# Moving z's gate into the next head's steps, and the key's sum of squares to two rounded passes

## The reference, cut to what matters

```python
def l2_normalize(x):
    return x * lax.rsqrt(jnp.sum(jnp.square(x), axis=-1, keepdims=True) + NORM_EPS)
def gated_deltanet_branch(qkv, z, b, a, conv_w, a_log, dt_bias, norm_g):
    ...
    qkv = jax.nn.silu(causal_depthwise_conv(front(qkv.astype(f32)), conv_w.astype(f32)))
    q, k, v = jnp.split(qkv, [GDN_QK, 2 * GDN_QK], axis=-1)
    ...
    k = l2_normalize(k.reshape(B, Lp, GDN_HEADS, GDN_DK))
    ...
    o = chunked_gated_delta_rule(bhl(q), bhl(k), bhl(v), bhl(g), bhl(beta))
    ...
    o = rms_norm(o, norm_g) * jax.nn.silu(z.astype(f32).reshape(B, L, GDN_HEADS, GDN_DV))
```

## Time and profile before

| | before |
|---|---|
| median of 3 runs | 2764.96 us (2764.6 to 2765.09) |
| the profiled execution | 2765.07 us, of which the span is 2763.3 us |
| TensorE busy (PE) | 2727.5 us, 99% of the span |
| VectorE busy (DVE) | 2018.0 us, 73% |
| ScalarE busy (ACT) | 1416.7 us, 51% |
| granted TensorE clock | 9 tenths or more in every slice |
| chain that ended last | PE 91%, DVE 6%, ACT 1%, issue 1% |

### The profile page before, as it was taken

How to read it: one execution, slowest core, us unless ns; L and a number is a source line. 1 busy time by engine, 2 the same in 40 slices (tenths; PEclk the granted TensorE clock), 3 DMA queues, 4 the chain that set the end, 5 groups by cost and what they waited for, 6 DMA issues and landing times.

```text
span 2763.3 us, 50816 instructions
## 1 busy us (share of the span) xinstructions
PE 2727.5 (99%) x17597; PEld 2459.0 (89%) x17597; DVE 2018.0 (73%) x3666; ACT 1416.7 (51%) x2453; POOL 310.5 (11%) x323
## 2 busy tenths in 40 slices
PE   7999999999999999999999999999999999999998
PEld 7999999999999888888888888888888998888887
DVE  7887888788788666667765666756777777788876
ACT  6556655655665434444443443534545555445553
POOL 0000000000000000004700000000470001500014
PEclk9999999999999999999999999999999999999999
DMA  5444444444444555556565555555555444554445
GB/s 218 151 154 140 156 140 158 138 148 154 144 152 134 182 185 190 187 188 219 173 197 190 182 192 183 192 195 182 195 179 175 165 168 160 184 166 144 144 156 182
DMA packets 130236, 472.74 MB, mean 171 GB/s; under 512 B 15136, under 2 KB 15136, under 8 KB 129952
## 3 DMA queue, kind: packets, MB, share of 16 engines
q1 hardware_dynamic: 126144, 457.37, 49.5%
q0 software_dynamic: 3936, 13.34, 1.6%
HBM read 468.40 MB, written 2.25 MB: 170 GB/s over the span
## 4 chain that ended last, share of the span: by engine, by line
PE 91%; DVE 6%; ACT 1%; issue 1%; DMA 0%; DVEq 0%; SPq 0%; ACTq 0%
PE bank L317 41%; PE bank L318 21%; PE bank L319 6%; PE bank L321 6%; PE bank L320 6%; DVE w_lo L293 2%; PE bank L888 1%; PE bank L843 1%; PE bank L897 1%; PE bank L1112 1%; PE bank L1272 0%; PE bank L955 0%; PE bank L1189 0%; DVE mix_f_bias L1909 0%; DVE mix_fq L2120 0%
## 5 line engine op out<-in xcount | busy, mean ns | idle before, releaser
L293 DVE TENSOR_TENSOR w_lo<-raw,w_hi 128x1024 fp32r<-128x1024 f32 x862 | 1058.5, 1253 | 135.0 <-ACT w_hi L287 132.0
L287 ACT ACTIVATE w_hi<-raw 128x1024 fp32r<-128x1024 f32 x862 | 896.5, 1052 | 434.1 <-PE bank L318 423.6
L317 PE MATMUL bank<-ya,w_hi 128*128 128x512 f32 x1792 | 625.4, 393 | 0.7 <-DVE h L2238 0.7
L317 PE MATMUL bank<-ux,w_hi 128*128 128x512 f32 x1744 | 621.3, 398 | 0.3 <-DVE w_lo L293 0.2
L318 PE MATMUL bank<-ya,w_lo 128*128 128x256 f32 x1792 | 501.4, 280 | 0.0
L318 PE MATMUL bank<-ux,w_lo 128*128 128x256 f32 x1744 | 488.1, 280 | 0.0
L319 PE MATMUL bank<-u,w_hi 128*128 128x272 f32 (+1 forms) x1296 | 410.0, 316 | 5.4 <-DVE u L444 3.5
L317 PEld LDWEIGHTS bank<-ya,w_hi 128*128 128x128 f32 x1792 | 336.6, 188 | 77.0 <-issue 2.2
L317 PEld LDWEIGHTS bank<-ux,w_hi 128*128 128x128 f32 x1744 | 327.6, 188 | 74.4 <-issue 2.9
L321 PE MATMUL bank<-u,w_lo 128*128 128x272 f32 (+1 forms) x1296 | 373.1, 288 | 0.0
L320 PE MATMUL bank<-u,w_hi 128*128 128x272 f32 (+1 forms) x1296 | 372.5, 287 | 0.0
(11 more groups left out here) (413 smaller groups left out, 3816.9 us busy)
## 6 DMA issues: line engine op xcount, KB each, us to landing
raw<-in_stream SPq DMA_DIRECT2D x864, 512.0 KB, 3.6
mix_row<-rows POOLq DMA_DIRECT2D x16, 408.0 KB, 4.7
xT<-in_xT SPq DMA_DIRECT2D x4, 544.0 KB, 5.5
mix_coef_m<-meta_rows POOLq DMA_DIRECT2D x16, 128.0 KB, 4.2
h<-in_xT POOLq DMA_DIRECT2D x1, 2048.0 KB, 9.8
out_dram<-h SPq DMA_DIRECT2D x8, 256.0 KB, 2.4
consts<-in_consts POOLq DMA_DIRECT2D x1, 1817.0 KB, 8.6
meta_rows<-mix_b_mat POOLq DMA_DIRECT2D x16, 1.0 KB, 3.0
```

Of the source, the lines that this page charges most:

```text
L287: act.activation(w_hi[:, slot], raw[:, slot], ACT.Copy).then_inc(hi_ready, 1)
L293: dve.tensor_tensor(w_lo[:, slot], raw[:, slot], w_hi[:, slot].bitcast(F32), ALU.subtract).then_inc(lo_ready, 1)
L317: pe.matmul(o, a, x, start=first, stop=False)
```

## The change

1. z's tanh and silu leave blocks 65 and 76 and stand at block 160, which is block 48 of the next head's window. The tanh is written into `z_silu` (and silu z reads it there) instead of `gate_th`. Head 16 has no next window: its two steps stay at 65 ("last tanh") and 76 ("last silu"), by way of `f_p`.
2. The table set for Ln and Exp is loaded after the key's tanh instead of after z's (in head 16 still after z's).
3. The key's squares are made twice by ScalarE: rounded (`k_sq_hi`, fp32r) and in full (`gate_th`). A new VectorE step `k rest` copies the ones into an fp32r tile `ones_r`, once per head since the tile lies where `both` is, and subtracts the high part from the full squares (`k_sq_lo`). `k sum` is now two fp32r matmuls of 272 columns.
4. The key's steps move up: silu k 68 to 63, k square 69 to 66, k rest at 66, k sum 80 to 74, turn 84 to 80, qk 87 to 82, kk 88 to 83. The sum of o's squares goes from 181 to 179, step 4 from 124 to 125.
5. Waits follow: the counts of "length sq" have one more per head, "o squared" becomes "squared" with three per head, `k root` of heads from 2 on waits for the root of o.

```diff
             def __init__(self, tag, spans):
-                self.tag, self.spans = tag, [list(s) for s in spans]
+                self.tag, self.spans, self.at = tag, [list(s) for s in spans], {}
...
             def __call__(self, name, shape, dt=F32):
...
+                        self.at[name] = s[0] - size
...
+        ones_r = place("ones_r", [P, P], F32R, mt.at["both"])
+        k_sq_hi = place("k_sq_hi", [P, TOK], F32R, mt.at["qk"])
+        k_sq_lo = place("k_sq_lo", [P, TOK], F32R, mt.at["th"])
...
         def norm_of_head(name, n):
...
-            (28, "columns"), (80, "k sum"), (84, "turn"), (87, "qk"), (88, "kk"), (96, "fq sum"), (97, "transpose"),
+            (28, "columns"), (74, "k sum"), (80, "turn"), (82, "qk"), (83, "kk"), (96, "fq sum"), (97, "transpose"),
...
+        def z_tanh(n):
...
+            return z_silu[:] if n < HEADS else f_p[:, 0:SEQ]
...
         def window(plan, head, size=HEAD, count=HEADS):
...
             def ones_sum(name, n, width):
...
-                pe.wait_ge(sem("length sq"), at_)
+                pe.wait_ge(sem("length sq"), at_ + n)
...
+                if name == "gdn k":
+                    pe.matmul(bank[2][:, :width], ones_r[:], k_sq_hi[:], start=True, stop=False)
+                    pe.matmul(bank[2][:, :width], ones_r[:], k_sq_lo[:], start=False,
+                              stop=True).then_inc(sem("length sum"), 1)
+                    return
...
+                if name == "gdn k" and n > 1:
+                    act.wait_ge(sem("length rs"), at_ - 1)
...
                 if x == "z":
-                    act.activation(gate_th[:, :SEQ], z_raw[:], ACT.Tanh, scale=0.5).then_inc(sem("silu tanh"), 1)
-                    act.preload_act_table_set("natural_log_exp_and_others")
+                    if n == HEADS:
+                        act.wait_ge(sem("fox p turned"), n - 1)
+                    elif n > 1:
+                        act.wait_ge(sem("gdn y"), 2 * (n - 1))
+                    act.activation(z_tanh(n), z_raw[:], ACT.Tanh, scale=0.5).then_inc(sem("silu tanh"), 1)
...
+                if x == ("k" if n < HEADS else "z"):
+                    act.preload_act_table_set("natural_log_exp_and_others")
...
             def act_k_square(n):
...
-                    act.wait_ge(sem("length rs"), norm_of_head("gdn o", n - 1))
-                square("gdn k", n, kT[:], TOK, 0.5)
+                    act.wait_ge(sem("gdn o"), 2 * (n - 1))
+                act.activation(k_sq_hi[:], kT[:], ACT.Square, scale=0.5).then_inc(sem("squared"), 1)
+                act.activation(gate_th[:], kT[:], ACT.Square, scale=0.5).then_inc(sem("squared"), 1)
...
             def act_q_square(n):
...
             def act_o_square(n):
...
-                act.activation(sq[:, :SEQ], bank[6][:, 0:SEQ], ACT.Square).then_inc(sem("o squared"), 1)
+                act.activation(sq[:, :SEQ], bank[6][:, 0:SEQ], ACT.Square).then_inc(sem("squared"), 1)
...
             def act_cols(n):
...
+                if n == HEADS:
+                    act.wait_ge(sem("silu"), 4 * n)
...
+            steps_act = {"columns": act_columns, "tanh": lambda n, x: (x != "z" or n < HEADS) and act_tanh(n, x),
+                         "last tanh": lambda n, x: n == HEADS and act_tanh(n, x), "k square": act_k_square, "cols": act_cols, "decay": act_decay,
...
                 if x == "z":
...
-                    dve.scalar_tensor_tensor(out=z_silu[:], in0=gate_th[:, :SEQ], scalar=1.0, in1=z_raw[:],
+                    dve.scalar_tensor_tensor(out=z_silu[:], in0=z_tanh(n), scalar=1.0, in1=z_raw[:],
...
+            def dve_k_rest(n):
...
+                if n > 1:
+                    dve.wait_ge(sem("v new"), 2 * (n - 1))
+                dve.tensor_copy(ones_r[:], const("ones")).then_inc(sem("length sq"), 1)
+                dve.wait_ge(sem("squared"), 3 * n - 1)
+                dve.tensor_tensor(k_sq_lo[:], gate_th[:], k_sq_hi[:].bitcast(F32), ALU.subtract).then_inc(
+                    sem("length sq"), 1)
...
             def dve_o_add(n):
-                dve.wait_ge(sem("o squared"), n)
+                dve.wait_ge(sem("squared"), 3 * n)
...
+            steps_dve = {"conv": dve_conv, "final": dve_final, "meta": dve_meta, "silu": lambda n, x: (x != "z" or n < HEADS) and dve_silu(n, x),
+                         "last silu": lambda n, x: n == HEADS and dve_silu(n, x), "g diff": dve_g_diff, "fox bias": dve_fox_bias,
...
-                         "o add": dve_o_add,
+                         "o add": dve_o_add, "k rest": dve_k_rest,
...
-                                dve.wait_ge(sem("length sq"), norm_of_head("gdn o", head))
+                                dve.wait_ge(sem("length sq"), norm_of_head("gdn o", head) + head)
...
```

More of the change, by code:

```diff
@@ L577, in program @@
         PE_PLAN = (
-            (28, "columns"), (80, "k sum"), (84, "turn"), (87, "qk"), (88, "kk"), (96, "fq sum"), (97, "transpose"),
+            (28, "columns"), (74, "k sum"), (80, "turn"), (82, "qk"), (83, "kk"), (96, "fq sum"), (97, "transpose"),
             (101, "prod", 1), (104, "fk sum"), (107, "step", 1), (110, "turn inverse", 1), (110, "prod", 2), (112, "step", 2),
             (115, "turn inverse", 2), (115, "prod", 3), (116, "logits"), (116, "turn v"), (117, "step", 3), (124, "turn inverse", 3), (124, "prod", 4), (124, "turn p"),
-            (124, "step", 4), (128, "turn inverse", 4), (128, "prod", 5), (128, "fox out"), (131, "step", 5), (135, "turn inverse", 5), (135, "prod", 6),
+            (125, "step", 4), (128, "turn inverse", 4), (128, "prod", 5), (128, "fox out"), (131, "step", 5), (135, "turn inverse", 5), (135, "prod", 6),
             (140, "meta v"), (142, "meta state"), (142, "step", 6), (144, "k state", 0), (148, "v new", 0),
-            (152, "state", 0), (167, "k state", 1), (169, "v new", 1), (171, "state", 1), (181, "o sum"))
+            (152, "state", 0), (167, "k state", 1), (169, "v new", 1), (171, "state", 1), (179, "o sum"))
         ACT_PLAN = (
-            (29, "columns"), (56, "tanh", "v"), (64, "tanh", "q"), (65, "tanh", "k"), (65, "tanh", "z"),
-            (69, "k square"), (72, "k root"), (79, "cols"), (81, "decay"), (83, "turned"), (90, "fq square"),
+            (29, "columns"), (56, "tanh", "v"), (64, "tanh", "q"), (65, "tanh", "k"), (65, "last tanh", "z"),
+            (66, "k square"), (72, "k root"), (79, "cols"), (81, "decay"), (83, "turned"), (90, "fq square"),
             (96, "fq root"), (99, "fk square"), (105, "fk root"), (116, "soft"), (120, "f v"), (126, "q square"),
[1 row of a table removed]
[1 row of a table added]
             (176, "o square"), (180, "o root"), (185, "y hi"))
@@ L591, in program @@
             (36, "conv", "v"), (49, "conv", "q"), (51, "silu", "v"), (60, "conv", "k"), (62, "silu", "q"),
-            (68, "silu", "k"), (71, "unit k"), (72, "g diff"), (72, "fox bias"), (76, "silu", "z"), (84, "decay b"),
+            (63, "silu", "k"), (66, "k rest"), (71, "unit k"), (72, "g diff"), (72, "fox bias"), (76, "last silu", "z"), (84, "decay b"),
             (86, "b mat"), (92, "qk"), (96, "level", 0), (98, "mask", 1), (99, "q dec"), (103, "unit fq"),
@@ L596, in program @@
             (127, "inverse turned", 4), (127, "mask", 5), (127, "meta", 1), (127, "f out"), (128, "level", 5), (128, "meta", 2), (129, "inverse turned", 5), (129, "final"),
-            (135, "mask", 6), (137, "level", 6), (142, "rhs", 0), (157, "state"), (168, "rhs", 1), (174, "o add"),
+            (135, "mask", 6), (137, "level", 6), (142, "rhs", 0), (157, "state"), (160, "silu", "z"), (168, "rhs", 1), (174, "o add"),
             (182, "y"), (184, "y lo"))
         HEAD = MIX_TILES * KT
+        def z_tanh(n):
+            return z_silu[:] if n < HEADS else f_p[:, 0:SEQ]
         def window(plan, head, size=HEAD, count=HEADS):
@@ L1491, in act_f_out @@
                                ACT.Copy).then_inc(sem("yb hi"), 1)
-            steps_act = {"columns": act_columns, "tanh": act_tanh, "k square": act_k_square, "cols": act_cols, "decay": act_decay,
+            steps_act = {"columns": act_columns, "tanh": lambda n, x: (x != "z" or n < HEADS) and act_tanh(n, x),
+                         "last tanh": lambda n, x: n == HEADS and act_tanh(n, x), "k square": act_k_square, "cols": act_cols, "decay": act_decay,
                          "k root": lambda n: root("gdn k", n, TOK, 1.0, ("gdn y", 2 * n - 2)),
@@ L2093, in dve_f_out @@
                                       sem("yb lo"), 1)
-            steps_dve = {"conv": dve_conv, "final": dve_final, "meta": dve_meta, "silu": dve_silu, "g diff": dve_g_diff, "fox bias": dve_fox_bias,
+            steps_dve = {"conv": dve_conv, "final": dve_final, "meta": dve_meta, "silu": lambda n, x: (x != "z" or n < HEADS) and dve_silu(n, x),
+                         "last silu": lambda n, x: n == HEADS and dve_silu(n, x), "g diff": dve_g_diff, "fox bias": dve_fox_bias,
                          "unit k": lambda n: unit("gdn k", n, kT, TOK, 0.5, "unit k"), "b mat": dve_b_mat,
```

(2 more changed lines are left out.)

## The result

The changed kernel takes **2751.68 us** (median of 5 executions, 2749.01 to 2752.13) against 2764.89 of the kernel before on the same chip: a ratio of 0.995, 95% interval 0.9938 to 0.9962, so 13.2 us or 0.48% faster. The profiled execution took 2749.95, its span is 2748.1 (2763.3 before). The forecast was 2749 us, a gain of 16.0 for the profiled execution; that one gained 15.1, and the median another 2 less.

A forecast was written before the change was run, and what follows sets the result against it. TensorE was taken as the bound, by what it executes and where it waits. Fifteen heads gaining 1.13 us each, less 0.9 lost in head 16, make 16.0 off 2765.07: 2749 us, range 2743 to 2759.

The forecast's parts named there:

- Fewer passes: At k sum, two fp32r matmuls take 0.25 us instead of 0.46 for one fp32: 0.21 gained per head.
- Block 48: z's tanh, table load and silu fit into idle time of ScalarE and VectorE there: cost 0, bounds 0 to 0.1 per head.
- The key's chain: Started earlier, it has 0.3 us slack at k sum and turn, so their waits of 0.13 and 0.31 go.
- rival A: The move is too tight: k sum's input is late in every head; priced at 2759 us, chance 12%.
- prod 1: At block 101, its 0.60 us wait for VectorE's level 0 goes; ScalarE's split of block 96 is late next.
- The new wait: At turn inverse 1, TensorE waits for level 1: 0.29 us lost per head with the restart, bounds 0 to 0.45.
- step 4: One block later, its 0.18 us wait for mask 4 goes; 0.17 per head is counted.
- Head 1: Gains at least 0.21 us and at most the whole sum per head; taken like the others at 1.13.
- Head 16: z's tanh stands ahead of the key's squares, so k sum waits 2.3 us with restart; the head loses 0.9.
- B: Nothing is won: the waits reappear at the same length along the level chain; 2764 us, chance 7%.
- C: Slower: table loads amid other work cost more than their row, twice 1.28 us giving 2780; chance 7%.
- fp32r costs as much as fp32: At k sum, the two rounded passes take 0.46 us and gain nothing; 2752 us, chance 0.08.

The follow-up runs named there:

- fp32_sum: The changed kernel with the key's sum as one fp32 matmul of one square again, no cast, no subtraction: 2753.11 us, ratio 0.9958.
- double_load: The changed kernel with a second table load behind the key's tanh in every head: 2765.89 us, ratio 1.0003.
- no_move_up: The changed kernel with k sum, turn, qk and kk back at blocks 80, 84, 87 and 88: 2753.86 us, ratio 0.996.
- late16: The changed kernel with the last head's z tanh moved from block 65 to 106 and its silu from 76 to 112: 2748.25 us, ratio 0.994.
- prod2_later: The changed kernel with prod 2 at block 111 instead of 110 and step 2 at 113 instead of 112: 2748.98 us, ratio 0.9941.
- both: The changed kernel with the edits of late16 and prod2_later together: 2745.94 us, ratio 0.9932.
- both3: As the run both, with prod 3 also moved from block 115 to 116, ahead of the logits: 2744.32 us, ratio 0.9926.

## Why the prediction was right, and where it was off

**What bounds the kernel** was right: TensorE with its waits. Pricing steps by starts, not by busy time, gave each term of the sum per head to within 0.04.

**Fewer passes**: 0.21 foretold, 0.21 measured in the ordinary heads of fp32_sum, with the wait of prod 2 unmoved. Right.

**Block 48**: cost 0, right. Conv q starts at 151.92 with the split before it just done, and `rhs` 1 starts 154.33, with no wait at its matmul (0.23 as before).

**The key's chain**: both waits went, 0.13 and 0.29 (0.31 was foretold). Its slack was mis-sized: 0.48 in the trace, 0.46 in double_load, 0.3 foretold, for the cast holds VectorE up by 0.14 and not by 0.29, its record overlapping the next one. The error was on the safe side, so rival A did not come up in the ordinary heads.

**prod 1**: 0.59 of 0.60, and the engine that is late next is the one named: VectorE waits for ScalarE's split of block 96 behind fq's root.

**The new wait**: 0.29 foretold and 0.29 measured, at prod 2 and not at turn inverse 1. The prediction didn't look at which of level 1's two outputs each of them reads.

**step 4**: 0.21 less 0.03 against 0.17. Right.

**Head 1** is the term that failed. I took it like the others (1.13) though I had bounds from 0.21 up; it gained nothing. Its prod 1 wait had been smaller (0.47 for the whole step, 0.23 left, 0.24 gained), turn gave 0.24 and step 4 0.21, but prod 2 cost 0.25, the step at block 30 of the next head 0.12, and k sum grew from 0.46 to 0.77. Counted from the start of block 64, `k_sq_lo` ends at 3.46 in head 3 and TensorE comes to k sum at 3.94; in head 1 it is 3.87 and 3.50. Two things are missing in head 1, both of an earlier head: the sum for o ahead of block 74 (0.44 of TensorE's work), and the steps at blocks 57 and 59 (0.23 each), without which TensorE comes to block 64 earlier against the key's chain. Each takes 0.4 from a slack of 0.48. Two runs bear it out: in head 1 of fp32_sum, with a shorter chain, k sum costs 0.46, which is no wait, and in head 1 of no_move_up, with k sum at block 80, it costs 0.25. The lower bound was wrong too: the same move that has slack in fourteen heads has none there.

**Head 16**: 2.3 foretold for the wait with its restart, 2.19 measured (k sum 2.44 for 0.25). The loss is 1.26 less 0.18 from step 4, so 1.1, against 0.9. The prediction credited head 16 with no new wait, since TensorE is late there, but prod 2 waits there as in every head (its group costs 0.63). The same mistake stands in the price of rival A, which has the 0.29 stay away once k sum is late: in double_load k sum is 0.82 later and the 0.29 is still there.

So in the profiled execution 15.1 against 16.0: head 1 gives 1.1 less, head 16 0.2 less, and 0.4 more comes from the rest. **The median** is 1.7 above that profiled execution because three of five executions show the lower mean clock of the trace that has the drop behind head 16's wait, which costs 1.6 there. The prediction took the wait for its length alone. In late16 both are gone with the wait: 1.8 of span, and the spread.

**The rivals.** A (the input late in every head) did not come up: slack 0.46 to 0.48; in head 1 alone the input is late. B (waits come back at the same length) is refuted: 0.29 of 1.4 came back, and fp32_sum shows that this wait doesn't grow when TensorE is faster. C (a table load that costs more) is refuted by double_load and by the 0.01 to 0.02 behind each load. That fp32r costs as much as fp32 is refuted by 0.25 against 0.46.

**What stays open**: why the clock falls in some executions behind head 16's wait and not in others of the same kernel. By the mean clock it fell in 10 of 15 executions of the kernels whose traces show 1.92 of idle time there (the changed one, twice, and prod2_later), in 8 of 10 with 3.21 (double_load), in none of 5 with 1.57 (fp32_sum), and in none of 15 without the wait (late16, both, both3). That ties it to the wait and leaves the rest unexplained.

## What to carry to other kernels

Price small steps on the bounding engine by the starts of its instructions, then ask of each wait which engine's chain sets it: a wait that hangs on the bounding engine's own earlier work moves along with it and takes nothing back, one that hangs on an independent chain would absorb the gain (fp32_sum shows the first; no run here tried the second by itself). Work out the first and the last pass of a loop by themselves, since the steps that give the others their slack may be missing there: here fourteen heads gained 1.13 us each, the first nothing, and the last lost 1.1, with 1.6 more through the clock in part of the executions. After a move, set the step that now waits one place later; three such edits of the order gave 7.4 us on top of 13.2.
